# A third Strassen block in ten gate and up pairs, with silu on ScalarE, in an fp32 decoder layer

## The reference, cut to what matters

```
D_FF = 5632                      # 11 groups of 512 columns
def swiglu(h, w_gate, w_up, w_down):
    return (jax.nn.silu(h @ w_gate) * (h @ w_up)) @ w_down
x = x + swiglu(rmsnorm(x, norm_ffn_g), w_ffn_gate, w_ffn_up, w_ffn_down)
```

## Time and profile before

| | us |
|---|---|
| median of 3 runs | 1743.13 |
| lowest, highest | 1742.66, 1743.29 |
| the profiled execution, its time | 1742.88 |
| its span, first to last instruction | 1740.6 |

### The profile page before, as it was taken

The page is one execution under the profiler, slowest core; times in us unless marked ns, Lnnn a source line. Parts: engine busy times, 40 slices in busy tenths (PEclk is TensorE's granted clock), DMA queues, the critical chain, the costliest instruction groups (busy, mean ns, idle before and its releaser), DMA issues.

```text
span 1740.6 us, 20479 instructions
## 1 busy us (share of the span) xinstructions
PE 1729.1 (99%) x7881; PEld 1435.1 (82%) x7881; DVE 1379.7 (79%) x1521; ACT 1002.8 (58%) x1248; POOL 29.8 (2%) x54
## 2 busy tenths in 40 slices
PE   9999999999999999999999999999999999999998
PEld 7888888888888888888888888888888888888886
DVE  7577677887888787888665589888888878888887
ACT  6767678554656565555465465555555545555554
POOL 1100000000000000000000000000000000000000
PEclk9999999999999999999999999999999999999999
DMA  9565665666566655556755456566666566566663
GB/s 339 175 201 163 216 183 161 200 213 199 183 193 196 194 179 183 178 169 220 266 183 192 149 156 202 185 194 195 195 200 218 192 209 197 179 195 196 212 194 118
DMA packets 176049, 338.24 MB, mean 194 GB/s; under 512 B 10704, under 2 KB 15312, under 8 KB 175696
## 3 DMA queue, kind: packets, MB, share of 16 engines
q1 hardware_dynamic: 173376, 327.98, 59.5%
q0 software_dynamic: 1296, 5.24, 1.0%
q10 hardware_dynamic: 1280, 3.71, 0.5%
HBM read 334.80 MB, written 2.10 MB: 194 GB/s over the span
## 4 chain that ended last, share of the span: by engine, by line
PE 98%; DVE 1%; ACT 0%; DMA 0%; issue 0%; ACTq 0%; POOLq 0%; POOL 0%; DVEq 0%
PE group L492 28%; PE group L494 28%; PE group L493 28%; PE side L492 3%; PE side L494 3%; PE side L493 3%; PE side L555 2%; PE side L662 0%; PE side L697 0%; DMA x_T_in<-in_x_T 0%; DVE w_lo L1284 0%; PE side L627 0%; PE side L626 0%; PE side L625 0%; DVE x_res L1639 0%
## 5 line engine op out<-in xcount | busy, mean ns | idle before, releaser
L876 ACT ACTIVATE w_hi<-w_raw 128x1024 fp32r<-128x1024 f32 x612 | 615.0, 1019 | 446.6 <-PE group L494 431.1
L1284 DVE TENSOR_TENSOR w_lo<-w_raw,w_hi 128x1024 fp32r<-128x1024 f32 x612 | 702.8, 1172 | 167.6 <-ACT w_hi L876 159.9
L492 PE MATMUL group<-w_hi,x_hi 128*128 128x512 f32 x1412 | 554.3, 393 | 0.8 <-DVE w_lo L1352 0.6
L494 PE MATMUL group<-w_hi,x_lo 128*128 128x512 f32 x1412 | 549.9, 389 | 0.0
L493 PE MATMUL group<-w_lo,x_hi 128*128 128x512 f32 x1412 | 549.5, 389 | 0.0
L492 PEld LDWEIGHTS group<-w_hi,x_hi 128*128 128x128 f32 x1412 | 265.1, 188 | 57.3 <-DVE w_lo L1284 2.6
L494 PEld LDWEIGHTS group<-w_hi,x_lo 128*128 128x128 f32 x1412 | 265.1, 188 | 55.6
L493 PEld LDWEIGHTS group<-w_lo,x_hi 128*128 128x128 f32 x1412 | 265.2, 188 | 53.4
L876 ACT ACTIVATE w_hi<-w_sums 128x1024 fp32r<-128x1024 f32 x114 | 121.1, 1062 | 210.1 <-PE group L494 173.7
L1284 DVE TENSOR_TENSOR w_lo<-w_sums,w_hi 128x1024 fp32r<-128x1024 f32 x114 | 139.4, 1224 | 97.1 <-ACT w_hi L876 97.1
L492 PE MATMUL group<-w_hi,inner_hi 128*128 128x512 f32 x274 | 107.0, 391 | 0.2 <-DVE x_res L1639 0.2
(11 more groups left out here) (336 smaller groups left out, 1897.4 us busy)
## 6 DMA issues: line engine op xcount, KB each, us to landing
w_raw<-in_w_in SPq DMA_DIRECT2D x223, 512.0 KB, 4.3
w_raw<-in_w_ffn_gate SPq DMA_DIRECT2D x88, 512.0 KB, 4.1
w_raw<-in_w_ffn_up SPq DMA_DIRECT2D x88, 512.0 KB, 4.6
w_raw<-in_w_ffn_down SPq DMA_DIRECT2D x88, 512.0 KB, 4.8
w_raw<-in_w_rnn_proj SPq DMA_DIRECT2D x32, 512.0 KB, 4.7
w_raw<-in_w_attn_proj SPq DMA_DIRECT2D x32, 512.0 KB, 4.7
w_raw<-in_w_mix_out SPq DMA_DIRECT2D x32, 512.0 KB, 4.8
w_raw<-in_w_xkv SPq DMA_DIRECT2D x16, 512.0 KB, 3.7
```

The source lines that it names most:

```text
L492: nc.tensor.matmul(out, h, whi[:, s, k, :], start=start, stop=False)
L494: return nc.tensor.matmul(out, l, whi[:, s, k, :], start=False, stop=stop)
L876: nc.scalar.activation(whi[:, s, ks], src[:, ks], ACT.Copy).then_inc(hi_ready[s], 1)
L1284: V_.tensor_tensor(wlo[:, s, ks], src[:, ks], whi[:, s, ks].bitcast(F32), ALU.subtract).then_inc(w_ready[s], 1)
```

## The change

In ten pairs (a1 to a5, b0 to b4) the plan becomes `O0 O2 W5 O4 W3 H6.0 W1 H7.0 H6.1 H7.1`: a third block of the eight is done by Strassen, and blocks 6 and 7 are cut into half steps (`H6.0` is the gate chunk of block 6, `H6.1` its up chunk). The positions are now 0 to 3 (O0, O2), 4 to 7 (W5), 8 and 9 (O4), 10 to 13 (W3), 14 (H6.0), 15 to 18 (W1), 19 to 21 (H7.0, H6.1, H7.1). The activation sums for the new block are made once, in pair a1 (VectorE at positions 4 and 7, ScalarE at 5); to have room, the buffer of the low parts grows by 2 KB. ScalarE computes silu itself, so L1720 goes; the scale buffer for it goes too. `weight_sums` can take A and B from raw buffers that aren't neighbours.

```diff
-UP_PLAN = "O0 O1 W3 O2 O4 W5 O6 O7".split()
+UP_PLAN = "O0 O2 W5 O4 W3 H6.0 W1 H7.0 H6.1 H7.1".split()
...
+        if step[0] == "H":
+            steps.append(("O", int(step[1]), int(step[3])))
+            continue
...
-            sums_made, inners = 4, 0
+            sums_made, inners = 5, 0
...
+                        if (part, j, kind, kp) == ("a", 1, "A", 1):
+                            pe.wait_ge(sem("sums_lo"), 5)
...
-                    last = nc.scalar.activation(silu[:, tt, :], fold[:, 0, tt, :], ACT.Tanh, scale=hrstd["x2"][:, tt:tt + 1])
-                last.then_inc(sem("tanh"), 1)
+                    last = nc.scalar.activation(silu[:, tt, :], fold[:, 0, tt, :], ACT.Silu, scale=rstd["x2"][:, tt:tt + 1])
+                last.then_inc(sem("silu"), 1)
...
+                        if (part, j, c) == ("a", 1, 5):
+                            sums_hi(us_hi[:, 0:1], up_sum[:, 0:1])
...
-                a = 2 * raw_of(m)[0]
-                then(V_.tensor_tensor(w_sums[:, :, 0, :], tiles[:, a:a + 4:3, :], tiles[:, a + 2:a + 3, :].to_broadcast([P, 2, GW]), ALU.add))
-                then(V_.tensor_tensor(w_sums[:, 1, 1, :], w_sums[:, 0, 0, :], tiles[:, a + 3, :], ALU.add))
+                a, b = 2 * raw_of(m)[0], 2 * raw_of(m + 1)[0]
+                if b == a + 2:
+                    then(V_.tensor_tensor(w_sums[:, :, 0, :], tiles[:, a:a + 4:3, :], tiles[:, a + 2:a + 3, :].to_broadcast([P, 2, GW]), ALU.add))
+                else:
+                    V_.tensor_tensor(w_sums[:, 1, 0, :], tiles[:, b + 1, :], tiles[:, b, :], ALU.add)
+                    then(V_.tensor_tensor(w_sums[:, 0, 0, :], tiles[:, a, :], tiles[:, b, :], ALU.add))
+                then(V_.tensor_tensor(w_sums[:, 1, 1, :], w_sums[:, 0, 0, :], tiles[:, b + 1, :], ALU.add))
...
-            def gate_silu():
-
-                made[0] += 1
-                dve.wait_ge(sem("tanh"), made[0])
-                marks["silu"] = marked(V_.scalar_tensor_tensor(silu[:, :, :], silu[:, :, :], 1.0, fold[:, 0], ALU.add, ALU.mult))
...
+                        if (part, j) == ("a", 1):
+                            if c == 4:
+                                then(V_.tensor_tensor(up_both[:, 0], xhi[:, 2:4, :].bitcast(F32), xlo[:, 2:4, :].bitcast(F32), ALU.add))
+                                sums_of(up_sum[:, 0:1], up_both[:, 0:1])
+                            if c == 7:
+                                sums_lo(us_lo[:, 0:1], up_sum[:, 0:1], us_hi[:, 0:1])
```

More of the change, by code:

```diff
@@ L79 @@
 A_SUMS = [int(_step[1:]) for _step in ATTN_PLAN if _step[0] == "W"]
-X_SUMS = [int(_step[1:]) for _step in UP_PLAN if _step[0] == "W"]
+X_SUMS = sorted(int(_step[1:]) for _step in UP_PLAN if _step[0] == "W")
 F_SUMS = {_part: sorted({int(_step[1:]) for (_of, _j), _plan in DOWN_PLAN.items() if _of == _part for _step in _plan if _step[0] == "W"})
@@ L242, in build @@
         xs_hi = at("x2_sums_hi", S + 12 * K1, [2, 4, P], F32R)
+        up_both, up_sum = at("up_both", S + 6 * K1, [3, CK, SEQ]), at("up_sums", S, [3, 4, P])
+        us_hi = at("up_sums_hi", S + 10 * K1, [3, 4, P], F32R)
         fs_hi, fs_lo = at("inner_sums_hi", U + 24 * K1, [4, 4, P], F32R), at("inner_sums_lo", V + 24 * K1, [4, 4, P], F32R)
-        STAGE = [region(4 * K1), region(4 * K1)]
+        STAGE = [region(4 * K1), region(6 * K1)]
         ks_hi = at("x_sums_hi", STAGE[0], [2, 4, P], F32R)
         xs_lo = at("x2_sums_lo", STAGE[1], [2, 4, P], F32R)
+        us_lo = at("up_sums_lo", STAGE[1], [3, 4, P], F32R)
         stage = [at(f"stage{n}", STAGE[n], [TT, GW]) for n in range(2)]
@@ L284, in build @@
         mem_parts = new("mem_parts", [TT, 2])
-        silu_scale = new("silu_scale", [TT])
         smax, nmax = new("smax", [TT, NB]), new("nmax", [TT, NB])
@@ L808, in _ @@
                     first = ("gate_" + part, j)
-                    for c, kind, kp in pair_of(first, xhi, xlo, xs_hi, xs_lo, X_SUMS):
+                    for c, kind, kp in pair_of(first, xhi, xlo, us_hi, us_lo, X_SUMS):
                         if c == 2 and (part, j) == ("a", 0):
@@ L1198, in _, with gate_silu @@
                         squares(xres, "x2", j - 1)
-            def gate_tanh(first):
+            def gate_silu(first):
                 wait_taken(act, GI[first])
                 for tt in range(TT):
-                    last = nc.scalar.activation(silu[:, tt, :], fold[:, 0, tt, :], ACT.Tanh, scale=hrstd["x2"][:, tt:tt + 1])
-                last.then_inc(sem("tanh"), 1)
+                    last = nc.scalar.activation(silu[:, tt, :], fold[:, 0, tt, :], ACT.Silu, scale=rstd["x2"][:, tt:tt + 1])
+                last.then_inc(sem("silu"), 1)
             def inner_split(kt0, summed):
@@ L1224, in _ @@
                             if c == 1:
-                                sums_hi(xs_hi[:, :, :, :], x_sum[:, :, :, :])
+                                sums_hi(us_hi[:, 1:3], up_sum[:, 1:3])
+                        if (part, j, c) == ("a", 1, 5):
+                            sums_hi(us_hi[:, 0:1], up_sum[:, 0:1])
                         if j > 0:
                             if c == 0:
-                                gate_tanh(("gate_" + part, j - 1))
+                                gate_silu(("gate_" + part, j - 1))
                             if c == 3:
@@ L1237, in _ @@
                         if c == 0 and q == 0:
-                            gate_tanh(("gate_" + part, groups - 1))
+                            gate_silu(("gate_" + part, groups - 1))
                         if c == 3 and q == 0:
@@ L1334, in _ @@
             ORDER = {"x1": 1, "x2": 2, "x3": 3}
[L1336 to L1339, removed]
             def lo_prologue():
@@ L1715, in _, with inner_tok @@
                         add_group(GI["cross_out", j], END["cross_out", j], j)
-            def gate_silu():
+            def inner_tok(second):
                 made[0] += 1
-                dve.wait_ge(sem("tanh"), made[0])
-                marks["silu"] = marked(V_.scalar_tensor_tensor(silu[:, :, :], silu[:, :, :], 1.0, fold[:, 0], ALU.add, ALU.mult))
-            def inner_tok():
-                dve.wait_ge(sem("vector_chain"), marks["silu"])
+                dve.wait_ge(sem("silu"), made[0])
+                wait_taken(dve, GI[second])
                 for tt in range(TT):
-                    last = V_.scalar_tensor_tensor(stage[0][:, tt, :], fold[:, 1, tt, :], silu_scale[:, tt:tt + 1], silu[:, tt, :], ALU.mult, ALU.mult)
+                    last = V_.scalar_tensor_tensor(stage[0][:, tt, :], fold[:, 1, tt, :], rstd["x2"][:, tt:tt + 1], silu[:, tt, :], ALU.mult, ALU.mult)
                 last.then_inc(sem("inner_tok"), 1)
@@ L1746, in _ @@
                                 variance("x2")
-                                halve("x2")
+                                dve.wait_ge(sem("rstd_x2"), 1)
                             if c == 0:
@@ L1750, in _ @@
                                 picked = [x[:, :, :].rearrange("p (j b) t -> p j b t", b=NB)[:, 1:3, 2:4, :].bitcast(F32) for x in (xhi, xlo)]
-                                then(V_.tensor_tensor(both[:, :, :, :], picked[0], picked[1], ALU.add))
-                                sums_of(x_sum, both)
+                                then(V_.tensor_tensor(up_both[:, 1:3], picked[0], picked[1], ALU.add))
+                                sums_of(up_sum[:, 1:3], up_both[:, 1:3])
                             if c == 2:
-                                sums_lo(xs_lo[:, :, :, :], x_sum[:, :, :, :], xs_hi[:, :, :, :])
+                                sums_lo(us_lo[:, 1:3], up_sum[:, 1:3], us_hi[:, 1:3])
+                        if (part, j) == ("a", 1):
[4 more added lines that the diff above has]
+                                sums_lo(us_lo[:, 0:1], up_sum[:, 0:1], us_hi[:, 0:1])
                         if j > 0:
                             if c == 0:
-                                gate_silu()
-                                inner_tok()
+                                inner_tok(("up_" + part, j - 1))
                             if c == 3:
@@ L1775, in _ @@
                         if c == 0 and q == 0:
-                            gate_silu()
-                            inner_tok()
+                            inner_tok(("up_" + part, groups - 1))
                         if c == 3 and q == 0:
```

## The result

The changed kernel takes 1747.37 us (median of 11 runs, 1746.83 to 1748.14), the kernel before 1742.96 beside it: ratio 1.0027, 95% interval 1.0018 to 1.0035. Slower, by 4.4 us or 0.3%. The profiled execution took 1747.27 us.

What follows compares the result with a forecast made beforehand. The prediction took TensorE as the bound, with every wait paid in full: 1742.88 - 6.80 + 4.9 + 4.7 + 1.45 = 1747.1, the median 0.25 above, so 1747.4 us. Range 1738 to 1752.

Steps and rivals of the forecast that it cites:

- What goes: TensorE in ten pairs: three matmuls fewer a pair at 0.2267 us each, 0.68 us a pair, 6.80 us saved.
- Place one: Position 10, A of the second block, seven pairs with down-product sums: TensorE waits 0.59 plus 0.11 us, 4.9 us total.
- the walk: Count through a pair of when each chunk is ready from VectorE and wanted by TensorE, giving the lateness at each place.
- Place two: Position 15, A of the third block, all ten pairs: TensorE waits 0.35 plus 0.11 us, 4.7 us total.
- Pair a1: New activation sums on VectorE at position 4 make chunks late: 1.92 us together, 1.45 beyond what was already counted.
- The refill: After a TensorE wait the second matmul comes 0.34 us later, not 0.227: 0.11 us more a wait, 2.1 over 19.
- the old wait at position 8: TensorE's existing wait at position 8, 0.07 and 0.11 us in a3, was to stay.
- fit there: Behind position 18: fold, joins, silu's multiplication and next sums have room; the next pair's A is 2.7 us early.
- Rival 1: All is covered: VectorE works ahead and A is in time at both places; 1736.3 us, faster; chance 0.13.
- Rival 2: One of the two places is covered, or both by half, a unit being too long; 1742.5 us; chance 0.25.
- Rival 3: The delay spreads: C is late too, 20 later blocks each pay some 0.2 + 0.11 us more; 1753; chance 0.12.

Runs made afterwards that it cites:

- e11: e10 with the third block's activation sums made inside pair a0, between its Strassen blocks, instead of ahead of a0; 1737.26 us against 1742.57 for the kernel before.
- e2: The changed kernel with only two Strassen blocks, one plain block between them and no third-block sums in a1; 1747.30 us against 1742.42 for the kernel before.
- e6: The changed kernel with one more 128x512 addition on VectorE ahead of A of the third block, in ten pairs; 1754.60 us.
- e10: e9 with D before C in all Strassen blocks and the third weight sum made behind A's split; 1737.93 us against 1742.78 for the kernel before.
- e5: The changed kernel with the down product's sums at positions 5, 8, 9 instead of 4, 5, 6, and a1's at 1, 2, 5; 1743.56 us.
- e3: The changed kernel with two plain chunks instead of one between the second and third Strassen block, one fewer behind the last; 1755.32 us.
- e4: The changed kernel with the sums for the down product made at positions 18, 19 and 20 instead of 4, 5 and 6; 1750.59 us.
- e8: The changed kernel with one more 128x512 addition on VectorE at position 21, behind the join that frees the bank, in ten pairs; 1747.14 us.
- e7: The changed kernel with one more 128x512 subtraction on VectorE at position 20, ahead of the join that frees the gate's PSUM bank, in ten pairs; 1755.95 us.
- e9: e5 with the down product's subtraction moved behind the join at position 21 and a1's sums made ahead of a0; 1741.06 us against 1742.78 for the kernel before.

## Why the prediction was right

The path was right: both places, their sizes and the pairs in which they stand came as forecast. That the total came within 0.1 to 0.2 us is partly luck: the parts counted came out 0.25 under the forecast, one item that the sum left out adds 0.6, and another takes off 0.3 (see *The sum*).

- *What goes.* 30 matmuls of 0.2267 us. It can't be measured bare in the changed kernel, but e11, with nearly all waits gone, is 5.3 us faster, and over the changed pairs its account closes (5.7 counted, 5.74 read). By the Trainium skill ("TensorE: Matmul & The Clock Gate", section "Back-to-back issue gap") they would be worth an estimated 6.5 us by its formula for a single gap, and an estimated 3.9 us by its 131 ns for a sustained stream. The rows have 226.7 ns, and e11's gain rules out the 3.9; from the times alone 6.5 can't be told from 6.8.
- *Place one* was 0.59 + 0.11 by the walk, and 0.59 to 0.61 + 0.11 in all seven pairs. e2 shows that the order alone costs it, 4.9 us for 4.9.
- *Place two* was 0.35 + 0.11, and 0.32 to 0.35 + 0.11 in nine pairs; e6 shows that it is VectorE's chain, one for one, and e10 that one addition fewer ahead of A takes it away.
- *Pair a1* was to cost 1.92 in all. The trace has 0.89 at position 8, 0.07 at A and 0.24 at C of the second block, 0.67 at place two: 1.87.
- *The refill* (the 0.11 behind a wait) stood at nearly every wait looked at, and was 0.08 at three: place two of a1, the first down product, and D of a1 in e5. The PE row of the waiting start is 0.50 long instead of 0.39. Behind the eight transposes, where the first start isn't late, the second one shows 0.09 of it too. The Trainium skill ("TensorE: Matmul & The Clock Gate", section "Step-by-step: what each phase is for") says that weight loads are pulled ahead of matmuls in flight when their row groups don't conflict or they go to the background weight buffer. In the gap-free stream the trace agrees: the load for the matmul at 1179.81 starts 0.22 us ahead of it. At a wait it doesn't, as the load starts together with its matmul, at 1178.78 in a3:

```profile
1178.78 0.19 PEld L497 LDWEIGHTS side<-w_hi,x_hi 128*128 128x128 f32 x1 [0.85 <-DVE w_lo L1293]
...
1179.59 0.19 PEld L498 LDWEIGHTS group<-w_lo,x_hi 128*128 128x128 f32 x1
```

- *The sum:* 7 x 1.15 + 2 x 0.45 + 1.87 = 10.8 of new waits less 6.8 = 4.0, where 4.25 was forecast and 4.35 is read over these pairs. Two items are missing in it. Behind each wait the next ten starts come a little slower than 0.2267 (0.23 to 0.236 for some of them), 0.01 to 0.06 us in all; over the new waits that is 0.6. And the old wait at position 8, which was to stay, shrank in a2 from 0.34 to 0.06, 0.3 less; in the other six pairs it stayed. Together 4.3.
- *Wrong in passing:* the fold and the joins "fit there". They did, with 0.17 us to spare. My walk looked at A of the next pair, 2.7 us early, and not at the PSUM bank that the next pair opens. That no wait came there was luck: the walk had not looked. The forecast was not touched by it, the first two repairs (e3, e4) failed by it. And L1720 was not worth nothing: about 0.5 us at the first down product.
- Rival 1 (all covered) needed VectorE to use its idle time; e8 against e7 shows that the idle is bound to places. Rival 2 needed a unit that was too long; both delays came out within 0.02 of the walk. Rival 3 had the right worry in the wrong place: outside a1 no C was late, and the small margin was that of the join.

## What to carry to other kernels

When two engines feed a third through a few buffers, list for each chunk and each buffer when it is wanted and when it is ready, and keep the smallest margins in sight, those of output banks too: here 0.7 us more of work a pair, on an engine with 3.4 us idle in it, cost nothing or nine us over ten pairs, depending on one step. Work that makes a saving possible belongs where its due time is far (e5, e9 and e11 have the changed kernel's additions in other places). What isn't needed by the first consumer should be done behind it (e10).

## What the runs showed of the hardware

In these traces a wait of TensorE cost more than its length when it ended at a 128x512 matmul with a new 128x128 weight. The following start came 0.33 to 0.34 us later instead of 0.227, after a wait of 0.05 us just as after one of 1.2 (at three waits 0.31), and the ten starts behind it another 0.01 to 0.06 us in all. Silu on ScalarE took 707 ns for 128x512, tanh 710. Silu needed one table load of 1283 ns for the whole stage, with copies and squares going on behind it without another load; the copy before the load, the load and silu followed each other within 0.03 us.
